# The second one-hot of the gate matrices, made on VectorE token by token

## What is computed

```python
def peer_ffn(x, w_query, sub_keys, down, up):
    bsz, seq, D = x.shape
    T = bsz * seq
    H, K, TB = PEER_HEADS, PEER_TOPK, PEER_TOKEN_BLOCK
    xt = x.reshape(T, D)
    q = (xt @ w_query).reshape(T, H, 2, PEER_HALF)
    s = jnp.einsum('thcd,cnd->thcn', q, sub_keys).astype(jnp.float32)
    sv, si = lax.top_k(s, K)
    cand_s = (sv[:, :, 0, :, None] + sv[:, :, 1, None, :]).reshape(T, H, K * K)
    cand_i = (si[:, :, 0, :, None] * PEER_NKEYS + si[:, :, 1, None, :]).reshape(T, H, K * K)
    top_s, pos = lax.top_k(cand_s, K)
    idx = jnp.take_along_axis(cand_i, pos, axis=-1)
    gate = jax.nn.softmax(top_s, axis=-1)

    def expert_block(args):
        xb, ib, gb = args
        a = jnp.einsum('thkd,td->thk', down[ib], xb).astype(jnp.float32)
        c = (gb * jax.nn.gelu(a)).astype(up.dtype)
        return jnp.einsum('thk,thkd->td', c, up[ib]).astype(x.dtype)
```

## Time and profile before

| | before |
|---|---|
| median of the runs | 2996.43 us (2987.22 to 2997.54) |
| the profiled execution: time, span | 2994.56 us, 2992.8 us |
| TensorE clock granted, mean of the span | 0.993 |
| TensorE busy (matmul) | 2938.1 us, 98% |
| VectorE busy | 2015.4 us, 67% |
| ScalarE busy | 1457.2 us, 49% |

### The profile page before, as it was taken

The page is one execution under the profiler, slowest core; times in us unless marked ns, Lnnn a source line. Parts: engine busy times, 40 slices in busy tenths (PEclk is TensorE's granted clock), DMA queues, the critical chain, the costliest instruction groups (busy, mean ns, idle before and its releaser), DMA issues.

```text
span 2992.8 us, 43948 instructions
## 1 busy us (share of the span) xinstructions
PE 2938.1 (98%) x17304; PEld 2601.5 (87%) x17304; DVE 2015.4 (67%) x3112; ACT 1457.2 (49%) x2280; POOL 14.6 (0%) x37
## 2 busy tenths in 40 slices
PE   8999999999999999999999999999999999999998
PEld 7888888889999888888888999988898998888997
DVE  6869998765555675999876555547665556665554
ACT  5531775544444453267545444445455444545443
POOL 0000000000000000000000000000000000000000
PEclk9999999999999999999999999999999999999999
DMA  5334546765544433445677555546555666554563
GB/s 185 104 128 155 171 167 210 258 248 196 196 170 181 144 107 111 155 159 173 204 235 264 210 182 188 194 135 176 182 171 172 188 187 184 174 182 143 149 190 134
DMA packets 223262, 528.52 MB, mean 177 GB/s; under 512 B 13466, under 2 KB 87360, under 8 KB 212096
## 3 DMA queue, kind: packets, MB, share of 16 engines
q1 hardware_dynamic: 221872, 521.11, 52.8%
q0 software_dynamic: 1232, 5.25, 0.5%
HBM read 507.42 MB, written 18.88 MB: 176 GB/s over the span
## 4 chain that ended last, share of the span: by engine, by line
PE 92%; DVE 6%; ACT 1%; issue 1%; DMA 0%; SPq 0%; POOL 0%; DVEq 0%; ACTq 0%; POOLq 0%
PE ps L2240 16%; PE ps L1240 14%; PE ps L2224 13%; PE ps L1290 12%; PE ps L1303 12%; PE ps L1274 11%; PE ps L553 3%; PE ps L562 2%; PE ps L1229 2%; PE ps L2484 1%; DVE ring_lo L536 1%; PE ps L656 1%; DVE arena L1512 1%; PE ps L1051 1%; PE ps L2407 0%
## 5 line engine op out<-in xcount | busy, mean ns | idle before, releaser
L1887 DVE TENSOR_TENSOR ring_lo<-ring,w_hi 128x1024 fp32r<-128x1024 f32 x320 | 388.9, 1224 | 271.0 <-ACT w_hi L1883 269.5
L1883 ACT ACTIVATE w_hi<-ring 128x1024 fp32r<-128x1024 f32 x320 | 336.7, 1057 | 270.8 <-PE ps L2240 184.2
L1240 PE MATMUL ps<-h_t,ring 128*128 128x256 f32 x2048 | 463.6, 379 | 0.9 <-ACT arena L885 0.9
L1240 PEld LDWEIGHTS ps<-h_t,ring 128*128 128x128 f32 x2048 | 379.8, 190 | 46.8 <-issue 1.3
L1290 PE MATMUL ps<-h_t_lo,down_hi 128*128 128x256 f32 x1024 | 288.6, 282 | 0.0
L1290 PE MATMUL ps<-h_t_expert,down_lo 128*128 128x256 f32 x1024 | 288.2, 281 | 0.0
L1290 PE MATMUL ps<-h_t_expert,down_hi 128*128 128x256 f32 x1024 | 287.1, 280 | 0.0
L2224 PE MATMUL ps<-h_t_hi,w_hi 128*128 128x256 f32 x928 | 260.4, 281 | 2.7 <-ACT arena L2039 2.7
L2224 PE MATMUL ps<-h_t_lo,w_hi 128*128 128x256 f32 x928 | 261.8, 282 | 0.0
L2224 PE MATMUL ps<-h_t_hi,ring_lo 128*128 128x256 f32 x928 | 260.0, 280 | 0.0
L1674 DVE TENSOR_TENSOR up_lo<-ring,up_hi 128x2048 fp32r<-128x2048 f32 x64 | 146.7, 2292 | 98.8 <-ACT up_hi L948 98.8
(11 more groups left out here) (446 smaller groups left out, 6697.4 us busy)
## 6 DMA issues: line engine op xcount, KB each, us to landing
ring<-in_peer_down SPq DMA_DIRECT2D x128, 1024.0 KB, 5.0
ring<-in_w_in SPq DMA_DIRECT2D x140, 512.0 KB, 3.7
ring<-in_peer_up SPq DMA_DIRECT2D x68, 1024.0 KB, 4.8
ring<-in_w SPq DMA_DIRECT2D x132, 512.0 KB, 3.8
ring<-in_peer_up SPq DMA_DIRECT2D x120, 512.0 KB, 4.3
arena<-late_gates SPq DMA_DIRECT2D x16, 1024.0 KB, 6.7
ring<-in_w_out SPq DMA_DIRECT2D x16, 512.0 KB, 3.6
ring<-in_peer_w_query SPq DMA_DIRECT2D x16, 512.0 KB, 4.6
```

The costliest lines, as they stand in the source:

```text
L1240: m = pe.e.matmul(PS[:, act_bank(b), j * T:(j + 1) * T], RING[:, b % 2, j * D + kc * P:j * D + (kc + 1) * P], HT[:, kc, :], start=kc == 0, ...
L1883: a.e.activation(W_HI[:, g % HI_SLOTS, :], RAW[:, g % RAW_SLOTS, :], ACT.Copy).then_inc(*a.count(f"c{g}_hi"))
L1887: v.e.tensor_tensor(RAW_LO[:, g % RAW_SLOTS, :], RAW[:, g % RAW_SLOTS, :], W_HI[:, g % HI_SLOTS, :].bitcast(F32), ALU.subtract).then_inc(* ...
```

## The change

VectorE makes both parts of HOT2, token by token: for each of the eight tokens and each of the two parts, one `tensor_scalar` on 128 x 128 that compares IOTA with the token's second key and multiplies by the gate's part, with both the key and the gate given as a scalar of each partition, read from SBUF (called a pointer scalar below). MASK is gone, and so are VectorE's two operations on it (L1640 and L1645), ScalarE's eight copies a group (L913), and the waits between the two engines for them. The sums wait for one mark, `hot<n>`. The low parts of the sums keep their places: one behind HOT1, one behind HOT2.

```diff
--- before.py
+++ after.py
@@ -337,8 +337,7 @@
         STAT = sb("stat", [P, 128])
         with nc.sbuf_tensor("one_hot", [P, 3072], F32) as ONE:
             pass
-        with nc.sbuf_tensor("hot_first", [P, 2, GROUP, P], F32R) as HOT1, \
-                nc.sbuf_tensor("hot_mask", [P, GROUP, P], F32) as MASK:
+        with nc.sbuf_tensor("hot_first", [P, 2, GROUP, P], F32R) as HOT1:
             pass
         with nc.sbuf_tensor("out_hi", [P, OUT_SLOTS, D], F32R) as OUT_HI:
             pass
@@ -903,17 +902,6 @@
                     a.e.wait_ge(*a.at("best_off"))
                     a.e.activation(BESTV, OFF, ACT.Exp).then_inc(*a.count("best_exp"))
 
-            def hot_high(n):
-
-                a.e.wait_ge(*a.at(f"mask{n}"))
-                if n >= 2:
-                    a.e.wait_ge(*a.at(f"sum{2 * n - 3}"))
-                for j in range(GROUP):
-                    at = n * GROUP + j
-                    a.e.activation(HOT2[n % 2][:, j, 0, :], MASK[:, j, :], ACT.Copy,
-                                   scale=PARTS[:, at, 0:1].bitcast(F32)) \
-                        .then_inc(*a.count(f"hot_high{n}" if j == GROUP - 1 else None))
-
             def gates_high(s):
 
                 if s // 2 >= STAGES and s % 2 == 0:
@@ -932,8 +920,6 @@
                 if n >= 2:
                     gates_high(2 * n - 3)
                     acts_out(2 * n - 3)
-                if n < GROUPS_OF_TOKENS:
-                    hot_high(n)
                 if n:
                     gates_high(2 * n - 2)
                     acts_out(2 * n - 2)
@@ -1220,8 +1206,7 @@
 
                 n, bank = s // 2, GATE_BANKS[s % 3]
                 if s % 2 == 0:
-                    pe.e.wait_ge(*pe.at(f"hot_low{n}"))
-                    pe.e.wait_ge(*pe.at(f"hot_high{n}"))
+                    pe.e.wait_ge(*pe.at(f"hot{n}"))
                 if s >= 3:
                     pe.e.wait_ge(*pe.at(f"low{s - 3}"))
                 for j in range(FEW):
@@ -1634,16 +1619,13 @@
                     .then_inc(*v.count())
                 if n >= 2:
                     gates_low(2 * n - 4)
-                if n:
-                    v.e.wait_ge(*v.at(f"hot_high{n - 1}"))
-                v.e.wait_ge(*v.mine(3 if n >= 2 else 1))
-                v.e.tensor_tensor(MASK[:, :, :], numbers, each(HK[:, 1, at:at + GROUP]), ALU.is_equal) \
-                    .then_inc(*v.count(f"mask{n}"))
+                for j in range(GROUP):
+                    for i in range(2):
+                        v.e.tensor_scalar(HOT2[n % 2][:, j, i, :], IOTA, HK[:, 1, at + j:at + j + 1],
+                                          PARTS[:, at + j, i:i + 1].bitcast(F32), ALU.is_equal, ALU.mult) \
+                            .then_inc(*v.count(f"hot{n}" if j == GROUP - 1 and i else None))
                 if n >= 2:
                     gates_low(2 * n - 3)
-                v.e.wait_ge(*v.at(f"mask{n}"))
-                v.e.tensor_tensor(HOT2[n % 2][:, :, 1, :], MASK[:, :, :], each(PARTS[:, at:at + GROUP, 1].bitcast(F32)),
-                                  ALU.mult).then_inc(*v.count(f"hot_low{n}"))
 
             def fold(n, w):
```

## The result

| | before | with the change |
|---|---|---|
| median | 2996.98 us (2987.22 to 3001.65, 4 runs) | 3096.22 us (3095.51 to 3097.64, 4 runs) |
| ratio | | 1.0335, 95% interval 1.032 to 1.0351 |
| span of the profiled execution | 2992.8 us | 3095.8 us |
| gates stage, layer 0 | 300.42 to 465.10: 164.68 us | 300.46 to 516.01: 215.55 us |
| gates stage, layer 1 | 1291.58 to 1456.28: 164.70 us | 1345.64 to 1561.17: 215.53 us |

The stage is counted from its first operation on VectorE (HOT1, or the mask where a version makes it first) to the first matmul at L1215, L1201 in the changed file.

The account below looks back on a forecast made before the run. VectorE (4.94 us a group) and TensorE (4.83) were both at their limit; VectorE's period becomes 6.52 us, adding 98.8 us in two layers plus 1.6 for the clock, 100 us on 2994.56, so 3096 us; range 3074 to 3142.

Parts of the forecast that it names:

- The bound: Gates stage before the change: VectorE sets 4.94 us a group, TensorE would need 4.83, so both are at their limit.
- that case: Rival for VectorE's sixteen operations: pointers cost nothing in a dense row, 0.14 us each, TensorE bounds, 2989 us; chance 0.04.
- The price of the new operation: VectorE's two-pointer operation on 128 x 128: 0.253 us start to start, sixteen of them 4.05 us a group.
- the forecast's own range: Whole kernel: 3082 to 3116 us, from 0.24 to 0.27 us start to start for each new operation.
- The period: VectorE's time a group in the gates stage: 2.47 us that stays plus 4.05 us added, 6.52 us against 4.94.
- the last step: End of the last group: its first sum waits for a low part, 0.33 + 0.42 us, and 0.1 us for the mark.
- The 0.20 us behind HOT1: VectorE's wait behind HOT1 for ScalarE's late high part: 0.20 us a group, dropped because ScalarE's copies ahead of it go.
- The tail: From the last group's first sum to the outputs at L1215: 7.9 us, unchanged, and the stage behind gives nothing back.
- The clock: TensorE's pauses lower its clock, which mostly fills the pause; 0.8 us a layer added at the stage's end, 1.6 in all.
- one pause of 1.7 us in each group: TensorE in the gates stage: idles 6.52 - 4.83 = 1.7 us a group, in one piece ahead of the group's first sum.
- The prediction's second rival: TensorE at 1.2 GHz for two thirds of the gates stage needs 7.2 us a group: 3141 us; chance 0.05.
- The rule that spoke for the change: VectorE's new operations: 58 cycles plus a cycle for two columns, 127 ns each, TensorE bounding, the kernel not slower.

Follow-up runs that it names:

- The version with seven tokens: Kernel before, mask ahead of HOT1 in every group, VectorE's product on seven tokens, ScalarE making the eighth's low part as a ninth copy: 2986.38 us, ratio 0.9957.
- the one with constants: Changed kernel with constants in place of both pointer scalars of the sixteen operations: 2984.33 us, ratio 0.9952 to the kernel before.
- the copies kept: Changed kernel with ScalarE's eight copies a group put back, into a tile that nobody reads: 3098.36 us, ratio 1.0327 to the kernel before.
- the version with the low part alone: Kernel before with HOT2's low part made by eight two-pointer operations in place of one product, mask and copies staying: 3039.25 us, ratio 1.013.
- the mask-first version: Kernel before with the mask made ahead of HOT1 in every group, ScalarE's order unchanged: 2994.40 us, ratio 0.9985.

## Why the prediction was right

The forecast was 3096 us, the median is 3096.22. The mechanism is the one forecast; that the sum met the median so closely is partly luck. Terms cancel, as shown below, and the medians lie 99.2 us apart where the two stages alone grew by 101.7, a difference within the spread of the kernel before (2987 to 3002 us). Point by point:

- **The bound.** Both engines at their limit, VectorE 4.94 us to TensorE's 4.83. The version with seven tokens and the one with constants bear it out: with VectorE under 4.83 us, TensorE sets the stage and the most that can be won is 4.6 us a layer (164.68 - 160.08). I had given 7 us in two layers for that case; it was 9, since the first sum also starts earlier.
- **The price of the new operation.** 0.253 us, from two pointers at 256 columns less 128 columns at 0.52 ns; measured 0.256. Both steps of that derivation were tested apart: 0.06 us a pointer, 0.067 us for 128 columns. (The top of the forecast's own range was worked out 3 us too high: p = 0.27 us gives 17 us more, 3113, not 3116.) I also said that one lasts about 0.345 us. That holds only for the shortest, 0.343; the middle one is 0.455 (smallest, middle and largest duration in ns in this row of the tile's view), since the recorded durations grew through the stage while the distance between starts stayed, as the last section shows:

```profile
L1624 DVE TENSOR_SCALAR hot_second<-common_sb,hk_t,gate_parts x1024: 343/455/630, 301.6 to 1551.8; 128x128 fp32r<-128x128 f32 x171
```

- **The period.** 2.47 + 4.05 = 6.52 us; measured 6.555, of which the sixteen are 4.10. The last group's first sum began 1.5 us later than worked out (508.09 for 506.6 us), each stage grew by 50.9 us in place of 49.4, and the two by 101.7 in place of 98.8. Of the 1.5 us, 1.1 had built up in the queue by the last HOT1 (501.01 for 499.9), and 0.4 came in the last step: the sum started 0.85 us after the low part it waits for, where 0.42 and 0.1 had been put down. These are the terms that were too small. TensorE's timeline of the changed kernel, that sum and the first matmul behind the stage:

```profile
508.09 0.71 PE L1214 MATMUL ps<-hot_second,hot_first 128*128 128x256 f32 x4 [1.93 <-DVE late_a L1606]
...
516.01 7.03 PE L1201 MATMUL ps<-ring,arena 128*128 128x512 f32 x16
```

- **The 0.20 us behind HOT1.** They went, as forecast, but not for the reason given, that ScalarE no longer has copies ahead of its high part. With the copies kept, HOT1 to the low part is 505.97 - 504.84 = 1.13 us too, and in the version with the low part alone 1.14. The longer period of VectorE is enough.
- **The tail.** From that sum to L1215 it is 516.01 - 508.09 = 7.92 us, as before (465.10 - 457.18). Nothing behind the stage gave time back.
- **The clock.** I added 0.8 us a layer for a stretch of low clock at the end of the stage; there was none of that (the tail is 7.92 us in both), and this term, 1.6 us too many, hid half of the 2.9 us that the period and the last step lacked. A slow stretch does fill the next pause, as TensorE's rows show (in brackets the idle time ahead). But it is rare: most pauses are like the one ahead of 501.52, with the matmuls behind it at full speed.

```profile
442.45 0.86 PE L1214 MATMUL ps<-hot_second,hot_first 128*128 128x256 f32 x4 [1.92 <-DVE late_b L1606]
443.10 3.45 PE L1225 MATMUL ps<-h_t,ring 128*128 128x256 f32 x8
...
446.86 1.89 PE L1225 MATMUL ps<-h_t,ring 128*128 128x256 f32 x8
449.01 0.71 PE L1214 MATMUL ps<-hot_second,hot_first 128*128 128x256 f32 x4 [0.26 <-DVE late_a L1606]
...
501.52 0.72 PE L1214 MATMUL ps<-hot_second,hot_first 128*128 128x256 f32 x4 [1.93 <-DVE late_a L1606]
502.07 1.89 PE L1225 MATMUL ps<-h_t,ring 128*128 128x256 f32 x8
```

After the pause of 1.92 us at 442.45 eight matmuls take 3.45 us in place of 1.89; the granted clock is 0.50 from 443.10 to 446.10 us, the lower of its two levels (1.2 GHz, against 2.4). What they lose comes off the next pause, which is 0.26 us, and VectorE doesn't notice: it has 150.00 of 150 us. In the two stages the timeline has 38 pauses of 1.9 us or more, and only eight of them are followed by a stretch at the lower clock; the prediction had such a stretch fill the pause most of the time. Nor is there one pause of 1.7 us in each group: nine quarters to four groups give mostly three of 1.92 us and a short one. The prediction's second rival needed the clock to stay low for two thirds of the stage, and the windows give 0.97 and 0.98.
- **The rule that spoke for the change.** By the Trainium skill (VectorE: DVE Perf Modes, section on the TRN2 errata) an operation on 128 columns in SBUF at two columns a cycle costs 127 ns by an estimate. With constants it measured 135 ns, so there the trace agrees to 6%; with two pointers it measured 256 ns, and there the measurement decides. The chance of 0.04 that I gave this case was for pointers that cost nothing in a dense row; the 1024 operations, in rows of sixteen, showed that they cost as much there.

## What to carry to other kernels

Before many small operations take the place of a few large ones, take the start-to-start time of the same form from the trace, and count its pointer scalars: here each cost 0.06 us, as much as 115 columns (at 0.52 ns). Fusing two steps lost here, since the fused form needs one instruction a token and part where the unfused one handled eight tokens at once; and it moved work from an engine busy for 114 of 150 us to one busy for 146. Where three engines feed one another in a ring with two buffers, shortening one wait can lengthen the next, so compare the length of the stage, not the wait.

## What was not expected

**Recorded durations of VectorE grew while its pace stayed.** The same low part, early and late in the changed kernel's stage of layer 0:

```profile
323.38 0.43 DVE L1605 TENSOR_TENSOR arena<-ps,arena 128x256 f32<-128x256 f32 x1
...
506.90 0.71 DVE L1605 TENSOR_TENSOR arena<-ps,arena 128x256 f32<-128x256 f32 x1
```

0.43 us has become 0.71, though operations start at the same distances, and TensorE starts on the mark later by about as much: 0.58 us after the start of the low part it waits for at 323.71 us, 0.85 us after the one at 507.24. After VectorE's first pause it is 0.43 us again. With ScalarE's copies kept it hardly grew (the last HOT1 of that version, the low part behind it, and the one behind the sixteen):

```profile
504.84 1.24 DVE L1630 TENSOR_TENSOR hot_first<-common_sb,hk_t 128x1024 fp32r<-128x1024 f32 x1
505.97 0.44 DVE L1617 TENSOR_TENSOR arena<-ps,arena 128x256 f32<-128x256 f32 x1
...
510.73 0.45 DVE L1617 TENSOR_TENSOR arena<-ps,arena 128x256 f32<-128x256 f32 x1
```

It isn't free. From the last HOT1 to the first sum behind it the changed kernel takes 508.09 - 501.01 = 7.08 us and the version with the copies 511.65 - 504.84 = 6.81, so the late mark costs 0.27 us at the end of the stage. The stages have the same length to 0.01 us only because the copies had cost VectorE's queue as much before (200.82 us to the last HOT1, against 200.55). What makes the durations grow wasn't tried.

**A wait for the engine's own last result costs VectorE 0.19 us** between two operations of 128 x 1024 (1.32 us start to start for 1.13) in the mask-first version, whose expectation had put it at 0.07 us. In the first group of the kernel before, where the product stands right behind the mask that it reads, it costs less:

```profile
301.55 1.22 DVE L1640 TENSOR_TENSOR hot_mask<-common_sb,hk_t 128x1024 f32<-128x1024 f32 x1
302.80 1.23 DVE L1645 TENSOR_TENSOR hot_second<-hot_mask,gate_parts 128x1024 fp32r<-128x1024 f32 x1
```

That is 1.25 us, so 0.12 above 1.13; why the two differ wasn't tried. In the later groups of that kernel two low parts stand between mask and product, and the product starts 0.33 us behind the second of them, without a wait.
